# Hybrid S5 / sparse-attention / mixture-of-experts block: thirteen gate tiles in three one-pass products, eight buffers for index scores, the causal mask in the first score step

## What is computed

```python
h = layer_norm(x)
u, q, k, v, q_idx, k_idx, w_idx, gate_pre = split(h @ w_in)   # gate_pre: 2 x 1024 columns
# index scores: 8 heads of 64; per block of 128 queries
dots  = einsum('bqhd,bsd->bhqs', q_idx, k_idx) * 64 ** -0.5
score = einsum('bqh,bhqs->bqs', w_idx * 8 ** -0.5, relu(dots))
score = where(causal, score, -inf)
_, sel = top_k(score, 128)                                    # keys kept for each query
g_ssm, g_att = split(sigmoid(gate_pre + b_gate))
mix = (g_ssm * y_ssm + g_att * y_att) @ w_o
h = layer_norm(alpha * h + mix)
h = layer_norm(alpha * h + moe(h))                            # top 4 of 32 experts
```

## Time and profile before

| | |
|---|---|
| median of 3 runs | 1735.17 us |
| lowest and highest run | 1733.05 and 1740.55 us |
| span of the profiled execution | 1738.5 us, 3.3 us above the median; no time outside the span is given for it |
| share of the span, PE, PEld, DVE, ACT, POOL | 96%, 63%, 86%, 61%, 27% |
| share of the chain of waits | PE 83%, DVE 12%, all else 5% |
| mean granted clock of TensorE | 0.980 of full speed |
| largest group in the changed part, L1571 | 256 passes, 111.5 us busy, 595 ns each from start to modelled end |

### The profile page before, as it was taken

One profiled execution on the slowest core, in us unless ns is written; L12 is line 12 of the kernel. 1 busy time (PEld: TensorE's weight loads), 2 busy tenths in 40 slices (PEclk: granted clock), 3 DMA queues, 4 the chain that ended last, 5 costly groups with the idle time before them and its releaser, 6 DMA issues.

```text
span 1738.5 us, 22182 instructions
## 1 busy us (share of the span) xinstructions
PE 1668.7 (96%) x7129; PEld 1088.9 (63%) x7129; DVE 1502.9 (86%) x1689; ACT 1062.2 (61%) x1015; POOL 466.9 (27%) x298
## 2 busy tenths in 40 slices
PE   4999999999998999999999999999999999999996
PEld 2333344466576577777777777777777777777763
DVE  5999886656667899999999999999999999999995
ACT  4323212266444577777777777777777777777771
POOL 4864200074533021122222121212222121211210
PEclk9998999999998999999999999999999999999997
DMA  5111113110407999999999999999999999999973
GB/s 174 49 52 49 49 49 121 49 69 30 142 37 263 375 353 361 361 364 376 366 368 362 372 377 355 370 357 376 368 363 360 373 376 365 365 361 377 378 277 106
DMA packets 91902, 464.76 MB, mean 267 GB/s; under 512 B 21290, under 2 KB 21406, under 8 KB 42617
## 3 DMA queue, kind: packets, MB, share of 16 engines
q1 hardware_dynamic: 80240, 441.67, 66.7%
q0 software_dynamic: 9776, 18.41, 4.3%
q10 hardware_dynamic: 1848, 4.24, 0.7%
HBM read 454.15 MB, written 18.53 MB: 272 GB/s over the span
## 4 chain that ended last, share of the span: by engine, by line
PE 83%; DVE 12%; issue 2%; ACT 1%; DMA 1%; POOL 1%; ACTq 0%; DVEq 0%; POOLq 0%
PE ps L1778 19%; PE ps L1780 19%; PE ps L1779 19%; PE ps L1571 6%; PE ps L1764 3%; DVE w_lo L1205 2%; PE ps L1498 2%; PE ps L1479 2%; PE ps L1493 2%; PE ps L1786 2%; PE ps L1487 1%; PE ps L1680 1%; PE ps L1681 1%; PE ps L1682 1%; DVE scr L1065 1%
## 5 line engine op out<-in xcount | busy, mean ns | idle before, releaser
L1205 DVE TENSOR_TENSOR w_lo<-raw,w_hi 128x2048 fp32r<-128x2048 f32 x384 | 873.7, 2288 | 73.1 <-ACT w_hi L838 71.9
L838 ACT ACTIVATE w_hi<-raw 128x2048 fp32r<-128x2048 f32 x384 | 737.0, 1919 | 239.1 <-PE ps L1780 237.8
L1778 PE MATMUL ps<-w_hi,x_hi 128*96 128x512 f32 x1024 | 414.1, 404 | 0.0
L1780 PE MATMUL ps<-w_lo,x_hi 128*96 128x512 f32 x1024 | 403.0, 394 | 0.0
L1779 PE MATMUL ps<-w_hi,x_lo 128*96 128x512 f32 x1024 | 402.2, 393 | 0.0
L1778 PEld LDWEIGHTS ps<-w_hi,x_hi 128*96 128x96 f32 x1024 | 168.2, 164 | 67.0 <-issue 2.0
L1778 PE MATMUL ps<-w_hi,a_hi 128*96 128x512 f32 x512 | 204.7, 400 | 5.7 <-DVE a_lo L1316 5.7
L1780 PEld LDWEIGHTS ps<-w_lo,x_hi 128*96 128x96 f32 x1024 | 165.3, 161 | 70.8
L1779 PEld LDWEIGHTS ps<-w_hi,x_lo 128*96 128x96 f32 x1024 | 165.9, 162 | 63.9
L605 POOL DMA_INDIRECT gate_now<-gate_rows,row_now x32 | 79.8, 2495 | 455.0 <-DVE tok_out L1346 439.9
L1779 PE MATMUL ps<-w_hi,a_lo 128*96 128x512 f32 x512 | 201.9, 394 | 0.0
(11 more groups left out here) (325 smaller groups left out, 2002.5 us busy)
## 6 DMA issues: line engine op xcount, KB each, us to landing
raw<-in_w_up SPq DMA_DIRECT2D x256, 1024.0 KB, 8.2
raw<-in_w_down SPq DMA_DIRECT2D x128, 1024.0 KB, 10.6
ring<-in_w_in SPq DMA_DIRECT2D x9, 2048.0 KB, 7.8
ring<-in_w_glu SPq DMA_DIRECT2D x4, 1024.0 KB, 6.2
ring<-in_w_o SPq DMA_DIRECT2D x2, 2048.0 KB, 11.7
h<-in_x SPq DMA_DIRECT2D x4, 512.0 KB, 5.6
ring<-in_w_attn_proj SPq DMA_DIRECT2D x1, 2048.0 KB, 8.1
h_rows<-h ACTq DMA_DIRECT2D x4, 512.0 KB
```

The lines of the kernel that those rows point to most:

```text
L838: s.activation(hi_of(c)[:, :], raw_of(c), ACT.Copy).then_inc(s_hi, 1)
L1205: d.tensor_tensor(lo_of(c)[:, :], raw_of(c), hi_of(c)[:, :], ALU.subtract).then_inc(s_lo, 1)
L1778: mm(o, xh, hi_of(c)[:, col], start=start, stop=False)
L1780: return mm(o, xh, lo_of(c)[:, col], start=False, stop=stop)
```

## The change

- The first three gate tiles stay as they are (`NATIVE = 3`). The other thirteen are computed as the GLU tiles are: 8 x 3 one-pass products each. For this the stream is split once: ScalarE copies `hT` into `h_hi` (eight copies of 128x512, `stream_upper`), GpSimd subtracts (`h_lo`). The weights of each tile are split by ScalarE (`gate_upper`, one copy of 128x1024 into one of two buffers) and GpSimd (the rest is written over the weights in their slot).
- The index scores have four buffers for the first block and eight for the two others; six of the eight lie over `hT`. So relu 10 waits until the third gate tile and the split of the stream are done.
- `causal`, a row block of 0 and -3e38 for each partition, is added in the first score step, which becomes a `scalar_tensor_tensor`. GpSimd's mask and VectorE's wait for it are gone. Query positions come from GpSimd; so do all of the first block's distances. `y_out(3)` moves to behind the ninth round of the first block.
- The order of gate tiles and scores is written out anew, and the load of the first layer norm's rows into `gb` moves behind the second GLU chunk, because `h_lo` lies in `gb`.

The core of the diff:

```diff
+            for n in range(KD):
+                pool.wait_ge(s_hhi, n + 1)
+                if n == 0:
+                    pool.wait_ge(s_stfree, SJ // 4)
+                g.tensor_tensor(h_lo[n // 4][:, n % 4, :], hT[:, n, :], h_hi[n // 4][:, n % 4, :], ALU.subtract)\
+                    .then_inc(s_hlo, 1)
+                pool.wait_ge(s_hlo, n + 1)
+
+            for n in range(NATIVE, 16):
+                pool.wait_ge(s_ghi, n - NATIVE + 1)
+                g.tensor_tensor(gate_lower(n), gate_weights(n), gate_hi[n % 2][:, :, :], ALU.subtract).then_inc(s_glo, 1)
+                pool.wait_ge(s_glo, n - NATIVE + 1)
...
-            def relus(n):
-                act.wait_ge(s_dot, n // 2 + 1)
-                if n >= 2:
-                    act.wait_ge(s_relufree, n - 1)
...
+            def relus(n0, n1):
+                for n in range(n0, n1):
+                    act.wait_ge(s_dot, n // 2 + 1)
+                    if 4 <= n < HEADS:
+                        act.wait_ge(s_relufree, n - 3)
+                    elif n >= HEADS:
+                        act.wait_ge(s_relufree, max(n - RELUS + 1, HEADS))
+                    if n == HEADS + 2:
+                        act.wait_ge(s_tile, first_tile["g"] + NATIVE)
+                        act.wait_ge(s_hlo, KD)
...
+            def gate_upper(g):
+                if g == NATIVE or g % 4 == 0:
+                    wait_chunk(act, 5 + g // 4)
+                if g >= NATIVE + 2:
+                    act.wait_ge(s_tile, first_tile["g"] + g - 1)
+                s.activation(gate_hi[g % 2][:, :, :], gate_weights(g), ACT.Copy).then_inc(s_ghi, 1)
...
+            for g in range(NATIVE, 16):
+                act.wait_ge(s_tile, first_tile["g"] + g + 1)
+                if g + 2 < 16:
+                    gate_upper(g + 2)
+                take(n + g)
+                if g == 4:
+                    relus(16, 20)
+                if g == 5:
+                    relus(20, 24)
+                    for q in range(4):
+                        gelu(q)
+                if g == 13:
                     act.wait_ge(s_far, TT - 1)
...
-                    src, wcol = relu[:, n % 2, 0:nk], wi[:, t, hh:hh + 1]
-                    if hh == 0:
-                        ins = d.tensor_scalar(sc, src, wcol, None, ALU.mult)
-                    else:
-                        ins = d.scalar_tensor_tensor(sc, src, wcol, sc, ALU.mult, ALU.add)
-                    ins.then_inc(s_relufree, 1)
+                    d.scalar_tensor_tensor(sc, relu_at(n), wi[:, t, hh:hh + 1], causal[:, SEQ - nk:] if hh == 0 else sc,
+                                           ALU.mult, ALU.add).then_inc(s_relufree, 1)
...
+                if g == NATIVE:
+                    pe.wait_ge(s_hlo, KD)
+                pe.wait_ge(s_glo, g - NATIVE + 1)
                 for k in range(KD):
-                    ins = mm(ps[n % 2][:, :], gate_weights(g)[:, k, :], hT[:, k, :], start=k == 0, stop=k == KD - 1)
+                    x_upper, x_lower = h_hi[k // 4][:, k % 4, :], h_lo[k // 4][:, k % 4, :]
+                    mm(o[:, :], gate_hi[g % 2][:, k, :], x_upper, start=k == 0, stop=False)
+                    mm(o[:, :], gate_hi[g % 2][:, k, :], x_lower, start=False, stop=False)
+                    ins = mm(o[:, :], gate_lower(g)[:, k, :], x_upper, start=False, stop=k == KD - 1)
```

More of the change, by code:

```diff
@@ L225, in build @@
         wg_lo = over("wg_lo", [P, 2, KD, 512], F32R, at_ring)
+        h_hi = [over(f"h_hi{r}", [P, 4, SEQ], F32R, at_scr, 2048 * b) for r, b in enumerate((12, 4))]
+        h_lo = [over("h_lo0", [P, 4, SEQ], F32R, at_gb), over("h_lo1", [P, 4, SEQ], F32R, at_scr, 2048 * 8)]
+        gate_hi = [over("gate_hi0", [P, KD, P], F32R, at_ring, 4 * 2 * CHUNK), over("gate_hi1", [P, KD, P], F32R, at_bias3)]
         u_hi = over("u_hi", [P, 4, SEQ], F32R, at_scr)
@@ L762, in _ @@
                 n += 1
-            g_done = 0
             act.wait_ge(s_st, SJ)
-            for i in range(24):
-                relus(i)
-                for _ in range(gates_after(i)):
-                    take(n)
-                    n += 1
-                    g_done += 1
-            for q in range(4):
-                gelu(q)
-            while tiles[n][0] == "g":
-                take(n)
-                n += 1
-                if g_done == 13:
+            relus(0, 4)
+            stream_upper(4, 6)
+            relus(4, 8)
+            stream_upper(6, 8)
+            take(n)
+            relus(8, 10)
+            gate_upper(NATIVE)
+            take(n + 1)
+            relus(10, 16)
+            gate_upper(NATIVE + 1)
+            take(n + 2)
+            for g in range(NATIVE, 16):
[10 more added lines that the diff above has]
+                if g == 13:
                     act.wait_ge(s_far, TT - 1)
@@ L1590, in _ @@
             gate_tile(n)
-            n += 1
             ymm(3)
-            for i in range(0, 24, 2):
-                if i >= 4:
-                    dots(i)
-                for _ in range(gates_after(i + 1) if i > 2 else 0):
-                    gate_tile(n)
-                    n += 1
-            while n < first_tile["gg"]:
-                gate_tile(n)
-                n += 1
+            dots(4)
+            dots(6)
+            gate_tile(n + 1)
+            dots(8)
+            dots(10)
+            gate_tile(n + 2)
+            dots(12)
+            dots(14)
+            gate_tile(n + 3)
+            gate_tile(n + 4)
+            dots(16)
+            dots(18)
+            gate_tile(n + 5)
+            dots(20)
+            dots(22)
+            for g in range(6, 16):
+                gate_tile(n + g)
+            n += 16
             def qk(i):
```

80 lines of the change are left out of this document (49 added, 31 removed).

## The result

The changed kernel takes 1722.8 us, the median of five runs (1721.2 to 1722.95), against 1737.1 for five runs of the kernel before that were measured with it (1733.05 to 1740.55). By the medians that is **14.3 us faster**. The ratio worked out over the runs is 0.9907, 95% interval 0.9893 to 0.9921, so 0.9% or 16 us, with an interval from 13.7 to 18.6 us. Forecast had been 1719, with a range of 1713 to 1728. The profiled execution took 1721.2 us with a span of 1719.4, 19.1 under the span that the prediction was worked out on.

The account below looks back on a forecast made before the run. TensorE, busy for 96% of the span, was taken as the bound. 18.1 us gained on thirteen gate tiles, less 1.3, 0.3 and 0.5, gives 16.0; from the 1735.2 median that is 1719, range 1713 to 1728.

Parts of the forecast that it names:

- The first term: Thirteen gate tiles on TensorE go from 90.2 to 72.1 us in one-pass products: 18.1 us gained.
- start-up: First product of a gate tile takes 0.43 instead of 0.23: 0 to 2.6 us lost over thirteen tiles, 1.3 taken.
- The small terms: Losses set against the gate tiles' gain: 1.3 us for slow first products, 0.3 for separated tiles, 0.5 for waiting score products.
- The wait at score products 14 and 15: TensorE waits there for relus 10 and 11, held until tile 2 ends: 0 to 1.0 us, 0.5 taken.
- the tightest: Weights' lower half for tile 4 ready at 262.6, where tile 3 ends at 263.3: 0.7 us to spare.
- the layout: VectorE's selections in the new order, tile by tile: third tile's last distances at 317.9, 14 us earlier than before.
- the collisions: Eight GpSimd subtractions falling on VectorE's score steps, 0.95 us each: 7.6 us, half the cover, nothing at the end.
- The rule of the Trainium skill named in the prediction: Shared ports locked for a whole instruction against two-input VectorE operations: eight subtractions cost 14.7 us, using all the cover.
- cover: VectorE's selections, due by 332.6 us before the GLU tiles, end at 317.9: 14.7 us to spare.
- Late halves: Rival, 0.12: with GpSimd subtractions of 5 us, some eleven gate tiles wait 0.6 each; 7 us back, 1726.
- The clock: Rival, 0.08: three more spells of TensorE's lower clock, in or behind the changed part, cost 5.4 us: 1724.6.
- The slower rival: Rival, 0.05: GpSimd blocks VectorE's search and replace rounds for 42.7 us; 28.0 lost, 16.0 gained, 1747.2.

Follow-up runs that it names:

- the tripled split: Changed kernel with three GpSimd operations of 128x1024 (subtract, add back, subtract) for each gate tile's lower half instead of one: 1747.5 us, ratio 1.0061.
- lengthened split: Changed kernel with two one-input GpSimd multiplications by 1.0 ahead of each gate tile's subtraction, measured on another chip: 1757.2 us, ratio 1.012.
- the second measurement: Changed kernel again with no edit, five rounds: 1722.3 us against 1738.75 for the kernel before, ratio 0.9895.

## Why the prediction was right

**The first term held.** Thirteen tiles of 24 products were put at 72.1 us, with 1.3 for start-up; they take 73.25. The products are 0.233 apart instead of 0.231, which is 0.6 us, and the start-up is 0.6 and not 1.3, since it appears only behind score products.

**The small terms held.** The wait at score products 14 and 15 was put at 0.5 and is 0.51. The stretch was to last 106.5 and lasts 106.4. The gain in it was to be 16.0, and is 16.1. (The 122.7 that the prediction sets beside the 106.5 reaches to GpSimd's split at 350.92; to the end of TensorE's part it is 122.5.) Tile 4, called the tightest, has its lower half at 261.6, where tile 3 ends at 263.0: 1.4 us to spare, not 0.7.

**VectorE: the layout was right, the collisions were priced too low.** Without collisions the last distances were put at 317.9; the measured 327.84 less the 10.7 counted above gives 317.1. The step that was off is the price of 0.95 us for each of the eight subtractions that fall on score steps, 7.6 us in all. The 0.95 came from a scan beside a 128x512 subtraction of 1.28, and half of the subtractions here are nearly twice as long. The losses scale with the other engine's instruction: 2.8 us in the four steps beside subtractions of 1.28, and 7.9 in what meets those of 2.4. Where the two engines take turns, a step lasts as long as the GpSimd instruction beside it, so it loses GpSimd's spacing less its own: 2.79 - 0.79 = 2.0 in the tripled split. The rule of the Trainium skill named in the prediction, a lock for a whole instruction, gave 14.7 us. Its kind is right, as the tripled split shows; its sum here is an upper end: a step lost about 2.0 to a subtraction of 2.4, and the last thresholds, which began when one was 0.9 us old, lost 1.3. Measured are 10.7, midway. One operation was missed entirely: the thresholds have one input and are stretched too, 0.43 to 1.77. The same section of the Trainium skill names `tensor_scalar`, which they are, among the operations that can enter a mode with both ports and then contend; the trace agrees with that, but does not show the mode. Of 14.7 us of cover 4.3 were left, so the error cost nothing.

**The rivals.** Late halves: not in the changed kernel, as GpSimd waits 2.7 us or more for ScalarE at every tile behind the first. It comes true in the tripled and the lengthened split, with 7.7 and 8.3 us of GpSimd a tile. The clock: 1.00 throughout the stretch; its spells behind it lengthen and shorten both kernels by a few us. The slower rival: refuted by the tripled split.

**The time.** 1719 was too low by 4 by the medians, though each term of the sum fits to within 0.7 us. Half of that, 1.9 us, is the ruler: the forecast is 16.0 under 1735.2, the median of three runs, and the five runs measured with the result have 1737.1. Later measurements of the kernel before have 1738.75 (seventeen runs), 1736.5 (sixteen) and 1737.35 (seven), so the ruler was short by 1 to 4 us. The other half is a gain of 14.3 by the medians where the trace shows 16.1, and that is inside what five runs can tell: the interval runs from 13.7 to 18.6. In the second measurement the medians give 16.4.

**The expected gain was not given back.** The kernel's later stages start 16.5 us earlier and stay so up to 503.5 us. From the last output projection to the last expert product it takes 1191.3 us before, and 1188.7 and 1191.3 in the two profiles of the changed kernel.

What stays open: why the spell of lower clock in the router has different lengths in executions of the same kernel, and why the first experts give back what a short spell saves. That the gains of two measurements differ by 2 us needs no cause; their intervals overlap.

## What to carry to other kernels

A part that frees a bound engine and a part that only makes room may each be worth nothing measurable alone; price them as one. When idle time of GpSimd is filled beside VectorE, count each instruction of VectorE that reads two operands, and each threshold, as lasting up to as long as the GpSimd instruction beside it, and compare the total with the cover at the next deadline. And set a predicted gain against the spread of the runs it is taken from before quoting a time: here every term of the sum was right to within 0.7 us and the time was off by 4.

## What was unexpected

- Score steps of 512 columns lose 2.0 us each beside a continuously busy GpSimd, but searches for the eight largest and replacements lose nothing (695 and 675 ns). Which operation a selection is built from decides whether it can lie beside GpSimd's work.
- The waiting goes both ways: a GpSimd cast of 0.61 us took 2.55 behind a VectorE subtraction.
- GpSimd needs 2.8 to 2.9 us for a one-input 128x1024 operation in place, over rows of 128 elements, and 2.41 for a two-input one on the same tile, while 128x512 with one input takes 0.69. Whether the rows or the writing in place make it so was not tried.
- Removing one collision hardly brought the end forward: two others, 20 and 85 us later, took the time back.
